# Seven block products instead of eight in the first layer's FFN output too, with their weight sums in the residual's place

## What is computed

```python
def swiglu(h, w_in, w_out):
    gate, up = jnp.split(h @ w_in, 2, axis=-1)
    return (jax.nn.silu(gate) * up) @ w_out
...
    mod = c_act @ ada_w[layer] + ada_b[layer]        # 6 vectors of 1024 per layer
    ...
    h = rms_norm(x, norm_g[layer, 2]) * (1.0 + sc_f) + sh_f
    y = swiglu(h, ffn_w_in[layer], ffn_w_out[layer])  # hidden width 2816
    x = x + (1.0 + ga_f) * rms_norm(y, norm_g[layer, 3])
```

## Time and profile before

| | us |
|---|---|
| runs of the kernel | 1370.5, 1370.72, 1374.61; median 1370.72 |
| profiled execution | 1369.45 |
| its span, first to last instruction | 1367.8 |
| PE busy | 1304.6 (95%) |
| DVE busy | 864.4 (63%) |
| ACT busy | 587.7 (43%) |
| POOL busy | 147.7 (11%) |
| layer 0's FFN, from its fourth tile to part 2's output products | 412.85 to 726.61 |
| its part 0 output products | 480.78 to 525.35 |
| its part 1, first quad to its end | 526.14 to 659.82 |
| layer 1's FFN, part 0 and part 1 output products | 1095.63 to 1136.01, 1223.05 to 1262.91 |

### The profile page before, as it was taken

The page is one execution under the profiler, slowest core; times in us unless marked ns, Lnnn a source line. Parts: engine busy times, 40 slices in busy tenths (PEclk is TensorE's granted clock), DMA queues, the critical chain, the costliest instruction groups (busy, mean ns, idle before and its releaser), DMA issues. The chain is left out here.

```text
span 1367.8 us, 18301 instructions
## 1 busy us (share of the span) xinstructions
PE 1304.6 (95%) x6963; PEld 1069.7 (78%) x6963; DVE 864.4 (63%) x1508; ACT 587.7 (43%) x1113; POOL 147.7 (11%) x160
## 2 busy tenths in 40 slices
PE   3799999999999999999999999999999999999998
PEld 3668788889798888888888876665887878887886
DVE  4879787557577655665655759776464564456235
ACT  3356674555453212221234665686352342333231
POOL 1002020005300000000000011120011001000000
PEclk9899999999999999999999999999999999999999
DMA  8654522110516555554532220010149479746121
GB/s 322 208 165 143 184 69 87 63 62 3 184 63 224 201 185 180 193 201 168 184 124 92 60 58 31 32 59 6 62 126 241 126 183 238 179 134 185 63 92 62
DMA packets 112456, 179.37 MB, mean 131 GB/s; under 512 B 9709, under 2 KB 74490, under 8 KB 112378
## 3 DMA queue, kind: packets, MB, share of 16 engines
q1 hardware_dynamic: 93018, 117.50, 26.2%
q0 software_dynamic: 19360, 60.82, 15.9%
HBM read 176.21 MB, written 2.10 MB: 130 GB/s over the span
## 5 line engine op out<-in xcount | busy, mean ns | idle before, releaser
L411 PE MATMUL ps<-h_hi,w_hi 128*128 128x512 f32 x872 | 344.7, 395 | 1.7 <-DVE w_lo L395 1.3
L413 PE MATMUL ps<-h_hi,w_lo 128*128 128x512 f32 x872 | 341.2, 391 | 0.0
L412 PE MATMUL ps<-h_lo,w_hi 128*128 128x512 f32 x872 | 341.0, 391 | 0.0
L395 DVE TENSOR_TENSOR w_lo<-raw,w_hi 128x1024 fp32r<-128x1024 f32 x156 | 189.3, 1222 | 182.6 <-ACT w_hi L389 182.0
L389 ACT ACTIVATE w_hi<-raw 128x1024 fp32r<-128x1024 f32 x158 | 165.3, 1051 | 98.5 <-PE ps L2387 69.7
L411 PEld LDWEIGHTS ps<-h_hi,w_hi 128*128 128x128 f32 x872 | 164.7, 189 | 36.0 <-ACT silu_g L2209 1.7
L413 PEld LDWEIGHTS ps<-h_hi,w_lo 128*128 128x128 f32 x872 | 164.6, 189 | 35.1
L412 PEld LDWEIGHTS ps<-h_lo,w_hi 128*128 128x128 f32 x872 | 164.8, 189 | 33.3
L514 DVE SCALAR_TENSOR_TENSOR ada_acc<-ada_in,c_act,ada_acc 128x512 f32<-128x512 f32 x154 | 115.5, 750 | 4.2
L2209 ACT ACTIVATE silu_g<-ps 128x512 f32<-128x512 f32 x44 | 26.2, 596 | 127.1 <-PE ps L413 117.6
L1070 DVE SCALAR_TENSOR_TENSOR tmp<-conv_u,conv_t,tmp 128x512 f32<-128x512 f32 x72 | 54.1, 752 | 35.0 <-ACT tmp L1064 32.9
(11 more groups left out here) (430 smaller groups left out, 2470.9 us busy)
## 6 DMA issues: line engine op xcount, KB each, us to landing
raw<-in_ffn_w_in_dram SPq DMA_DIRECT2D x44, 1024.0 KB, 6.1
ada_in<-in_ada_w_dram POOLq DMA_DIRECT2D x40, 1024.0 KB, 5.6
raw<-in_gdn_w_in_dram SPq DMA_DIRECT2D x16, 1024.0 KB, 5.8
raw<-in_ffn_w_out_dram SPq DMA_DIRECT2D x16, 1024.0 KB, 5.1
ada_in<-in_ffn_w_out_dram POOLq DMA_DIRECT2D x14, 1024.0 KB, 10.3
raw<-in_ffn_w_out_dram SPq DMA_DIRECT2D x12, 512.0 KB, 3.6
ada_in<-in_ada_w_dram SPq DMA_DIRECT2D x4, 1024.0 KB, 9.4
x_t<-in_x_dram SPq DMA_DIRECT2D x2, 2048.0 KB, 10.2
```

The source lines that it names most:

```text
L395: ops.tensor_tensor(lo, raw_tile(s, kc) if src is None else src, f32(hi), ALU.subtract).then_inc(lo_done, 1)
L411: nc.tensor.matmul(out_, hi[:, k, :], r_hi[:, k, :], start=k == 0, stop=False)
L412: nc.tensor.matmul(out_, hi[:, k, :], r_lo[:, k, :], start=False, stop=False)
L413: last = nc.tensor.matmul(out_, lo[:, k, :], r_hi[:, k, :], start=False, stop=k == kc - 1)
```

## The change

`SEVEN = (0, 1)`: layer 0's parts 0 and 1 make seven products too. `ada_in` is taken by slabs there, so the sums "three" and "four" go to `x_sum`, which lies where `x_t` is. `x_t` is written to a buffer off the chip (`x_kept`) before the FFN and read back behind part 1. POOL's list is `first_seven_pool`. In both layers the seven products come in a new order, one of them is read twice into `y_ffn` (sixteen `seven_y` instructions per part, fourteen before), the `raw` halves are loaded once with a block each, and the adds of `add_two` go on top of them after their splits. The plain output products of layer 0's part 0 and 1 are gone, with DVE's `dve_y`.

```diff
-    SEVEN = (1,)
+    SEVEN = (0, 1)
...
+        x_sum = [fixed(f"x_sum{i}", [P, 4, 512], at=x_at + 8192 * i) for i in range(2)]
+        W_SUM = [x_sum, ada_in]
+        ALL = [[fixed(f"all_{part}{layer}", [P, 2, 1024], F32R, at=at + 8192 * i) for i, part in enumerate(("hi", "lo"))]
+               for layer, at in enumerate((x_at, ada_base))]
...
+                if m == 1 and b == 0:
+                    dve.wait_ge(sem("x_kept"), 32)
...
         def seven_sp(sp, layer, p):
-            sp.wait_ge(lo_done, u - 2)
-            sp.dma_start(as_quarter(raw[0]), quarter(layer, p, 0, 0)).then_inc(raw_in[0], 16)
-            sp.wait_ge(lo_done, u)
-            sp.dma_start(as_quarter(raw[1]), quarter(layer, p, 1, 0)).then_inc(raw_in[1], 16)
             for side in range(2):
-                for k in (0, 2):
-                    sp.wait_ge(lo_done, u + 2 * side + k // 2 + 1)
-                    sp.dma_start(as_quarter(raw[side])[:, k:k + 2, :], quarter(layer, p, 0, side)[:, k:k + 2, :])\
+                sp.wait_ge(lo_done, u - 2 + 2 * side)
+                for k0, k1 in ((0, 2), (2, 3), (3, 4)):
+                    sp.dma_start(as_quarter(raw[side])[:, k0:k1, :], quarter(layer, p, side, side)[:, k0:k1, :])\
                         .then_inc(raw_in[side], 16)
             sp.wait_ge(lo_done, u + 6)
-            sp.dma_start(w_sum[0][:, :, :], quarter(layer, p, 1, 1)).then_inc(sem("last_in"), 16)
+            sp.dma_start(W_SUM[layer][0][:, :, :], quarter(layer, p, 1, 0)).then_inc(sem("last_in"), 16)
...
+        def add_two(pool, layer, p, side):
+            q, n, _ = part_quads(layer, p)
+            added(pool, as_quarter(raw[side]), quarter(layer, p, 0, 1), sem(f"two_in{side}"),
+                  lo_done, 4 * (q + n) + 2 * side + 2)
...
+        def first_seven_pool(pool):
+            pool.wait_ge(sem("h_mm"), turn_no(0, NB - 1, 1))
+            pool.dma_start(x_kept, flat(x_t[:, :, :])).then_inc(sem("x_kept"), 16)
+            pool.wait_ge(sem("x_kept"), 16)
+            for p in range(2):
+                if p:
+                    load_ada(pool, 1, 4)
+                    pool.wait_ge(sem("all_used"), 1)
+                begin_pool(pool, 0, p)
+                load_ada(pool, p, (11, 5)[p])
+                add_three(pool, 0, p, 0)
+                add_four(pool, 0, p, 0)
+                add_three(pool, 0, p, 1)
+                add_four(pool, 0, p, 1)
+                load_ada(pool, 1, 6 * p)
+                add_four(pool, 0, p, 2)
+                load_ada(pool, 1, 6 * p + 1)
+                load_ada(pool, 1, 6 * p + 2)
+                add_two(pool, 0, p, 0)
+                add_two(pool, 0, p, 1)
+                load_ada(pool, 1, 6 * p + 3)
+            load_ada(pool, 1, 10)
+            pool.wait_ge(sem("all_used"), 2)
+            pool.dma_start(flat(x_t[:, :, :]), x_kept).then_inc(sem("x_kept"), 16)
+            load_ada(pool, 1, 11)
...
-            product(4, plain(0, 0), ring(0), True, read_to(read - 2), split_to(0), made(1))
-            product(6, plain(1, 0), ring(1), True, read_to(read - 12), split_to(2), made(2))
+            product(4, plain(0, 0), ring(0), True, first_free, split_to(0), made(1))
+            if layer == 0:
+                pe_ada(pe, 13 + 6 * p)
+                if p == 0:
+                    pe.wait_ge(sem("ffn_mul"), 2 * (c0 + n))
+                    pe_cb(pe, 1, 2)
+            product(0, mixed(2), ring(1), True, gates_read, split_to(2), made(4))
             product(4, mixed(1), ring(0), False, read_to(read), split_to(4), made(3))
-            product(2, mixed(0), ring(1), True, bank_two, split_to(6), made(3))
+            product(2, mixed(0), ring(1), True, ups_read, split_to(6), made(3))
             product(4, plain(0, 1), ring(0), False, read_to(read + 4), split_to(8), made(1))
-            product(2, mixed(2), ring(1), False, read_to(read + 6), split_to(10), made(4))
-            product(4, plain(1, 1), summed, False, read_to(read + 8),
-                    lambda j: pe.wait_ge(sem("all_lo"), 2 * p + j + 1), made(2))
+            if layer == 0:
+                pe_ada(pe, 14 + 6 * p)
+            product(0, plain(1, 0), ring(1), True, read_to(read + 2), split_to(10), made(2))
+            product(4, plain(1, 1), summed, False, read_to(read + 10),
+                    lambda j: pe.wait_ge(sem("all_lo"), 2 * done + j + 1), made(2))
...
-                            if layer in SEVEN and isinstance(i, int) and i == 0 and p and s >= 2:
-                                pe.wait_ge(sem("seven_read"), 14 * (p - 1) + 11 + s % 2)
+                            if layer in SEVEN and isinstance(i, int) and i == 0 and p:
+                                pe.wait_ge(sem("seven_read"), 16 * part_no(layer, p - 1) + (13 if s < 2 else 9) + s % 2)
...
-            load_ada(pool, 0, 11)
-            repeat(pool, 12, lambda j: load_ada(pool, 1, j))
+            first_seven_pool(pool)
```

More of the change, by code:

```diff
@@ L106, in build_trunk @@
     N_FFN = sum(p // 2 + 2 for p in PARTS)
-    SEVEN = (1,)
-    N_SEVEN = N_FFN + 2
-    Q_DSA = Q_FFN[0] + N_FFN
+    SEVEN = (0, 1)
+    N_FFN = [N_FFN + 2 if layer in SEVEN else N_FFN for layer in range(2)]
+    Q_DSA = Q_FFN[0] + N_FFN[0]
     Q_DSA_OUT = Q_DSA + 3
@@ L1908, in part_quads, with low_quads @@
             return q, PARTS[p] // 2, layer * (FC // 2) + F0[p] // 2
+        def low_quads(layer, p):
+            before = sum((PARTS[2] if x in SEVEN else FC) // 2 for x in range(layer))
+            return before if layer in SEVEN else before + F0[p] // 2
         def ffn_sp(sp, layer):
@@ new lines, in added, with begin_pool, add_three @@
+        def added(pool, dst, block, signal, before, here):
+            pool.wait_ge(before, here)
+            pool.dma_start(dst, block, accum_op=ALU.add).then_inc(signal, 16)
+        def begin_pool(pool, layer, p):
+            for i, signal in enumerate(("three_in", "four_in")):
+                pool.dma_start(W_SUM[layer][i][:, :, :], quarter(layer, p, 0, 0)).then_inc(sem(signal), 16)
+        def add_three(pool, layer, p, k):
+            j, d = ((0, 1), (1, 1))[k]
+            added(pool, W_SUM[layer][0][:, :, :], quarter(layer, p, j, d), sem("three_in"),
+                  sem("three_in"), 48 * part_no(layer, p) + 16 * k + 16)
@@ L1972, in seven_pool @@
                 else:
[L1973 to L1979, removed]
@@ L1980, in seven_pool @@
-                add(four, sem("four_in"), 64 * p + 48, 1, 0, p)
-                here = 16 * (q + n) + 48
-                for side in range(2):
-                    add(as_quarter(raw[side]), sem(f"two_in{side}"), here, side, 1, p, raw_in[side])
-        def seven_src(layer, p, q, s):
[L1987 to L1992, removed]
-            return (src, sem("three_in"), 48 * p + 48) if a == 1 else (src, sem("last_in"), 16 * p + 16)
+                    pool.wait_ge(sem("all_used"), part_no(layer, p))
@@ new lines, in seven_pool @@
+                begin_pool(pool, layer, p)
+                for k in range(2):
+                    add_three(pool, layer, p, k)
+                    add_four(pool, layer, p, k)
+                add_four(pool, layer, p, 2)
+                for side in range(2):
+                    add_two(pool, layer, p, side)
+        x_kept = nc.dram_tensor("x_kept", (P, NB * D), F32, kind="Internal").ap() if 0 in SEVEN else None
+        def first_seven_pool(pool):
[23 more added lines that the diff above has]
+            load_ada(pool, 1, 11)
@@ L2200, in ffn_act @@
                 seven = layer in SEVEN and p < 2
-                l0 = layer * (FC // 2) if layer in SEVEN else c0
+                l0 = low_quads(layer, p)
                 def epilogue(i, s):
@@ L2230, in ffn_act @@
                 if seven:
+                    if layer == 0 and p == 0:
+                        act_cb(act, 1, 2)
                     for s in range(4):
```

117 lines of the change are left out of this document (72 added, 45 removed).

## The result

The changed kernel takes 1386.0 us (median; 1385.0 to 1387.4) against 1370.7 of the kernel before on the same chip: ratio 1.0101, 95% interval 1.0082 to 1.0119. It is **slower by 1%**, 15 us beyond the forecast and outside its range. Its profiled execution took 1386.55, the span 1384.8, the granted clock 0.981 (0.988 before).

The account below looks back on a forecast made before the run. PE (95% busy) was taken as the bound, with DVE deciding the rest. Terms -10.9 - 3.5 + 0.5 + 3.3 + 2.1 + 2.0 + 5.9 + 1.5 = +0.9 on 1369.45 gave 1371 us, range 1360 to 1380.

Parts of the forecast that it names:

- Matmuls: Layer 0's two parts lose 24 matmuls each, 48 at 0.2267 us: -10.9.
- Layer 1: PE's waits of 2.02 and 1.51 ahead of layer 1's fifth products go, as nothing is reloaded: -3.5.
- The second product's margin of 0.8: Layer 1's new second product needs the last mixed block at 1103.1, made 1102.3; costs nothing unless that margin goes.
- Start of layer 0's FFN: The 2 MB write of `x_t` shares DMA engines with SP's first two loads; slab-10 wait bounded 0 to 2: +0.5.
- Slab 12 behind four adds: Layer 0, part 0: slab 12 lands at 456 and 459, DVE waits 5, PE is late at its turn: +3.3.
- +2.1 and +2.0: DVE still behind at part 0's first product, +2.1; the same list behind slab 16 in part 1, +2.0.
- the prediction's own sign: The prediction is wrong if slab 12 lands before DVE asks for it, or DVE idles during layer 0's seven products.
- Seven products in layer 0: DVE late with the sixth product's splits and the read freeing bank 0, +5.9; leftovers of slabs 15 and 21, +1.5.
- B: Rival: adds run near 8.4, not 13.6, so slabs come in time: 1364, or 1361; chance 0.34.
- C: Rival: first pair of adds lands at 17.4, not 13.6, at slabs 12 and 18: 1379; chance 0.30 with D's end.
- D: Rival: layer 1 keeps its waits, the add's landing being set by other traffic: +3.5, 1374.5; its end shares C's 0.30.
- The DVE wait for `ada_in` in the third quad: Sign in either part of layer 0: about 5 us, against 0 for B and over 8 for C.

Follow-up runs that it names:

- run 3: Changed kernel with layer 0's 14 adds cut to 128x64 numbers each, all in their places: 1365.6 us, ratio 0.9942 to the kernel before.
- run 1: Changed kernel with seven products in layer 1 only, layer 0 as before: 1368.2 us, ratio 0.9971 to the kernel before.
- run 11: run 8 with the 2 MB write of `x_t` held until SP's first `w_in` load of quad 1 has landed: 1359.9 us, ratio 0.9914.
- run 6: Changed kernel with five adds per part for seven, in both layers, and one begin load per part fewer: 1362.5 us, ratio 0.9919 to the kernel before.
- run 12: Changed kernel with its seven adds, layer 0's first four per part each waiting for the landing of the one before: 1390.8 us, ratio 1.0124.
- run 9: run 8 with DVE doing the two splits for the sixth product ahead of the second pair of reads of bank 2: 1361.5 us, ratio 0.9916.
- run 10: Changed kernel with slab 12 (18) ahead of the second pair of adds in POOL's queue, slab 13 ahead of the last: 1395.3 us, ratio 1.0171.
- run 4: Changed kernel with PE turning slabs a tile later in layer 0's parts 0 and 1, DVE taking them in its last two steps: 1387.6 us, ratio 1.0106.
- run 8: run 6 with each part's begin load issued behind slab 11 (17) instead of ahead of it: 1361.3 us, ratio 0.9919 to the kernel before.

## Why the prediction was wrong, point by point

- **Matmuls, -10.9**: the 48 are gone (run 3 and the count); right.
- **Layer 1, -3.5**: right; 4.1 from trace to trace and 4.0 in run 1. The second product's margin of 0.8 held.
- **Start of layer 0's FFN, +0.5 (bounds 0 to 2)**: mis-sized. Slab 10's wait went from 0.94 to 4.09, and the first full tile came 0.7 later: +3.8. The write took 7.1 and not 10.2, yet the split of SP's first load is 1.8 late beside it (407.20 for 405.43), and run 11 takes 1.15 of the wait away. The adds have no part in it: with their bytes gone (run 3) it is 4.26. With one begin load for two (run 6) it is 2.57. A late load passes through DVE's order into the slab's sums, a step that the bound left out.
- **Slab 12 behind four adds, +3.3, and with it +2.1 and +2.0**: this is **the step that failed**. The adds' landings were as taken: issued at 424.20, landed by 436.5 and 443.6, the later one of the second pair by 457.3. But the step followed only POOL's queue. It priced SP's load in the same stretch at "451 with a late load", 1 us, where 2 MB had to pass at 0.078 MB/us. The trace of the kernel before had nearly that rate, 0.082: this is its DMA view of 1030 to 1042, layer 1, with two adds in flight.

```profile
q0 software_dynamic: 917, 1.81, 81.4%
q1 hardware_dynamic: 974, 0.98, 29.5%
```

  So the late thing was `w_in`, by 9, and slab 12, landed at 460.6, came while DVE was late anyway: DVE asked for it at 464.17. By the prediction's own sign (it is wrong if slab 12 lands before DVE asks for it) this decides. Measured: 6.13 + 5.00 + 0.54 at the slabs' turns, 1.70 + 1.57 + 0.18 in the first products, 15.1 against 7.4. A wait of the forecast kind exists: run 12 has it (15.08), where the adds don't starve SP but four single ones in a row make the slab 13 us later than in the changed kernel.
- **Seven products in layer 0, +5.9 and +1.5**: right in kind, too large. 0.75 + 1.81 ahead of the sixth, 0.58 + 0.60 at bank 0, 0.28 + 0.31 at slabs 15 and 21: 4.3 against 7.4. That DVE is the bound there is shown by run 9.
- **The clock**: not in the sum at all, about +5.

Together, from the forecast's +0.9: +3.3 for the start, +7.7 for the quads, -3.1 for the seven products, +5.1 for the clock and -0.6 for layer 1 give 13.3; measured are 17.1 for the profiled execution. Of what is left, 1.6 is the way waits are counted: idle time begins 0.39 after a matmul's start and not 0.23, in ten more places than before. The 2 that remain are in small places and weren't followed.

**The rivals.** B (the slabs in time) lost its premise, since the adds took 13.4 and not 8.4; DVE waited for no slab all the same, as B says, with the opposite result. C had the sign and nearly the size (1379 and, with the full price twice, 1387), through another transfer. D fell. The range's upper end, 1380, rested on the first pair landing at 17.4; no bound was drawn for SP's queue. Of what the prediction said would show it, these came true: 48 matmuls fewer, no idle start ahead of layer 1's fifth products, POOL's first add near 421 (424), slab 12's loads later (by 14 and 15, with 20 forecast), and idle time ahead of the sixth products. That the splits ended it is shown by run 9; the profile names no one there. The DVE wait for `ada_in` in the third quad, and PE's behind it, did not.

## What to carry to other kernels

When DMAs are added to one queue, ask what the other queues get beside them: count both queues' packets and their sizes in a short stretch, and put the rate against what the next consumer needs. Then lay them out one at a time between the transfers with due times. The same seven adds cost 20 us more as pairs in a row than spread singly, and the faster kernel has the higher DMA share, 0.98. Neither half of that is enough: spread but in pairs (run 10) the kernel is slower than the changed one, singly but in a row (run 12) no faster. A late input is paid where an in-order engine next owes something to the bottleneck, so moving that debt (run 4, run 9) gains nothing while the engine has no slack.

## What was not expected of the hardware

- An add's packet of 2 KB holds a DMA engine as long (0.170 us) as 3.9 KB of plain load (0.165 us).
- Two queues got one packet each in turn, whatever their sizes (925 and 923 beside adds, 614 and 620 beside plain loads). So the one with 1 KB packets had a third of the bytes beside adds and a fifth beside plain loads, at the same 0.078 MB/us.
- After PE idle times of 4.09 and 6.13 the granted clock stood at half for 3.1 and 3.5 us of full work. After one of 2.63 (run 8) it was 1.00 over 421 to 424, after 2.57 (run 6) 0.55: near that length it went either way.
